# First attention of a two-block model: the value products of two macros issued together every second step, out of four buffers of turned tiles

## What is computed

```python
def forgetting_attention_mixer(h, w_q, w_o, k, v, log_f_cum):
    q = (h @ w_q).reshape(b_sz, t_len, FOX_HEADS, FOX_HD).transpose(0, 2, 1, 3)
    for blk in range(t_len // FOX_QBLOCK):              # four blocks of 128 queries
        s = jnp.einsum("bhqd,bhkd->bhqk", q[:, :, s0:e], k[:, :, :e]) * scale
        s = s + log_f_cum[:, :, s0:e, None] - log_f_cum[:, :, None, :e]
        p = jax.nn.softmax(jnp.where(mask, s, -jnp.inf), axis=-1)
        outs.append(jnp.einsum("bhqk,bhkd->bhqd", p.astype(v.dtype), v[:, :, :e]))
    return o.transpose(0, 2, 1, 3).reshape(b_sz, t_len, FOX_WIDTH) @ w_o
```

## Time and profile before

| | us |
|---|---|
| median of 3 runs (lowest to highest) | 1696.85 (1696.52 to 1697.41) |
| the profiled execution, its own time | 1696.14 |
| its span, first to last instruction | 1694.3 |
| PE busy | 1669.6 (99%) |
| DVE / ACT / POOL busy | 585.4 / 652.6 / 689.0 |
| steps 2 to 19 of the first attention (start of S(2) to start of the tile of step 20) | 863.69 to 928.24 |

### The profile page before, as it was taken

The page is one execution under the profiler, slowest core; times in us unless marked ns, Lnnn a source line. Parts: engine busy times, 40 slices in busy tenths (PEclk is TensorE's granted clock), DMA queues, the critical chain, the costliest instruction groups (busy, mean ns, idle before and its releaser), DMA issues.

```text
span 1694.3 us, 23544 instructions
## 1 busy us (share of the span) xinstructions
PE 1669.6 (99%) x9382; PEld 1401.0 (83%) x9382; DVE 585.4 (35%) x1173; ACT 652.6 (39%) x987; POOL 689.0 (41%) x538
## 2 busy tenths in 40 slices
PE   6999999999999999999999999999999999999999
PEld 6787889898888888897977898888888887887887
DVE  3459325440100001411256230100011536788661
ACT  4653624442222222522456342222222545544651
POOL 3533333434444455535322434544455433554002
PEclk9999999999999999999999999999999999999999
DMA  5212110422222322232120222222322222222001
GB/s 199 75 64 87 51 53 23 162 76 99 99 99 99 111 98 88 75 137 100 52 98 2 75 75 99 84 98 93 125 99 99 100 100 99 75 95 80 26 2 50
DMA packets 23427, 145.00 MB, mean 86 GB/s; under 512 B 3504, under 2 KB 4272, under 8 KB 7344
## 3 DMA queue, kind: packets, MB, share of 16 engines
q1 hardware_dynamic: 23344, 143.83, 24.2%
HBM read 141.72 MB, written 2.10 MB: 85 GB/s over the span
## 4 chain that ended last, share of the span: by engine, by line
PE 68%; issue 13%; POOL 10%; DVE 5%; ACT 2%; DMA 1%; SPq 0%; POOLq 0%; ACTq 0%; DVEq 0%
POOL wlo L2839 10%; PE PS L452 5%; PE PS L454 5%; PE PS L453 5%; PE PS L485 4%; PE PS L343 4%; PE PS L346 4%; PE PS L338 4%; PE PS L487 4%; PE PS L486 4%; PE PS L961 2%; PE PS L466 2%; PE PS L467 2%; PE PS L468 2%; PE PS L1642 2%
## 5 line engine op out<-in xcount | busy, mean ns | idle before, releaser
L2839 POOL TENSOR_TENSOR wlo<-wraw,whi 128x512 fp32r<-128x512 f32 (+1 forms) x476 | 628.4, 1353 | 903.1 <-ACT whi L145 903.1
L145 ACT ACTIVATE whi<-wraw 128x2048 fp32r<-128x2048 f32 (+1 forms) x119 | 225.7, 1896 | 240.0 <-PE PS L346 182.7
L452 PE MATMUL PS<-hT_hi,whi 128*128 128x512 f32 x704 | 274.0, 389 | 0.0
L453 PE MATMUL PS<-hT_lo,whi 128*128 128x512 f32 x704 | 273.9, 389 | 0.0
L454 PE MATMUL PS<-hT_hi,wlo 128*128 128x512 f32 x704 | 273.9, 389 | 0.0
L1544 DVE TENSOR_TENSOR act_sb<-sil,PS 128x512 f32 x44 | 30.3, 688 | 428.5 <-ACT sil L1519 428.5
L1519 ACT ACTIVATE sil<-PS 128x512 f32<-128x512 f32 x44 | 26.4, 599 | 355.2 <-PE PS L454 335.4
L452 PEld LDWEIGHTS PS<-hT_hi,whi 128*128 128x128 f32 x704 | 132.1, 188 | 27.8 <-issue 0.6
L453 PEld LDWEIGHTS PS<-hT_lo,whi 128*128 128x128 f32 x704 | 132.2, 188 | 27.4
L454 PEld LDWEIGHTS PS<-hT_hi,wlo 128*128 128x128 f32 x704 | 132.1, 188 | 27.4
L485 PE MATMUL PS<-whi,hT_hi 128*128 128x512 f32 (+2 forms) x288 | 112.3, 390 | 0.1
(11 more groups left out here) (412 smaller groups left out, 3036.4 us busy)
## 6 DMA issues: line engine op xcount, KB each, us to landing
wraw<-wpack SPq DMA_DIRECT2D x125, 1024.0 KB, 4.9
gain<-gains SPq DMA_DIRECT2D x10, 512.0 KB, 6.5
x_sb<-x SPq DMA_DIRECT2D x8, 512.0 KB, 6.8
out<-x_sb SPq DMA_DIRECT2D x3, 512.0 KB, 2.6
csb<-consts SPq DMA_DIRECT2D x1, 704.0 KB, 13.4
out<-x_sb SPq DMA_DIRECT2D x2, 256.0 KB, 2.0
vh<-vecs SPq DMA_DIRECT2D x1, 96.0 KB, 6.4
small<-vecs SPq DMA_DIRECT2D x1, 80.0 KB, 11.4
```

The source lines that it names most:

```text
L145: act.activation((whi[q % 2] if static is not None else hi_of_slot(n))[:, w], wraw[q % 2][:, w], ACT.Copy).then_inc(w_hi, 1)
L452: nc.tensor.matmul(o, whi[q][w], hT_hi[:, k, :], start=(k == 0), stop=False)
L453: nc.tensor.matmul(o, whi[q][w], hT_lo[:, k, :], start=False, stop=False)
L2839: p.tensor_tensor(lo[:, a:b], wraw[q][:, a:b], hi[:, a:b].bitcast(F32), ALU.subtract).then_inc(w_lo, 1)
```

## The change

`fpt` has four buffers in place of two. The two new ones lie at 52 and 56 KB of the arena. Step m of PE issues no values where m is even; where m is odd, it issues V(m - 3) and then V(m - 2), without anything between them. A copy into `fpt[m % 4]` waits for V(m - 4). Nothing is added or taken away on any engine; ACT, DVE, POOL and SP keep their order.

```diff
-        fpt = [at(f"fpt{i}", AT_XN + 4 * KB * i, [P, 2, SEQ]) for i in range(2)]
+        fpt = [at(f"fpt{i}", (AT_XN if i < 2 else AT_ARENA + 44 * KB) + 4 * KB * i, [P, 2, SEQ]) for i in range(4)]
...
-                                            fpt[m % 2][:, r, c + j * P:c + (j + 1) * P], start=(j == 0), stop=(j == i))
+                                            fpt[m % 4][:, r, c + j * P:c + (j + 1) * P], start=(j == 0), stop=(j == i))
...
                     for p in self.ended(m - 2):
                         if m <= self.n:
                             self.pe_sums(p)
-                    if 0 <= m - 2 < self.n:
+                    if m % 2 and m >= 3:
+                        self.pe_values(m - 3)
                         self.pe_values(m - 2)
...
             def copy_ready(self, eng, m, r):
                 eng.wait_ge(sem("fx_turned"), 2 * m + r + 1)
-                if m >= 2:
-                    eng.wait_ge(sem("fx_pv"), m - 1)
+                if m >= 4:
+                    eng.wait_ge(sem("fx_pv"), m - 3)
```

More of the change, by code:

```diff
@@ L1883, in act_copy @@
                     self.copy_ready(a, m, 1)
-                    a.activation(fpt[m % 2][:, :, :], PS[:, self.turned[0]:self.turned[0] + 2, :], ACT.Copy).then_inc(sem("fx_pt_a"), 1)
+                    a.activation(fpt[m % 4][:, :, :], PS[:, self.turned[0]:self.turned[0] + 2, :], ACT.Copy).then_inc(sem("fx_pt_a"), 1)
                 if self.copies[m] == "av":
                     self.copy_ready(a, m, 0)
-                    a.activation(fpt[m % 2][:, 0, :], PS[:, self.turned[0], :], ACT.Copy).then_inc(sem("fx_pt_a"), 1)
+                    a.activation(fpt[m % 4][:, 0, :], PS[:, self.turned[0], :], ACT.Copy).then_inc(sem("fx_pt_a"), 1)
             def dve_copy(self, m):
@@ L1892, in dve_copy @@
                     self.copy_ready(v, m, 1)
-                    v.tensor_copy(fpt[m % 2][:, :, :], PS[:, self.turned[0]:self.turned[0] + 2, :]).then_inc(sem("fx_pt_v"), 1)
+                    v.tensor_copy(fpt[m % 4][:, :, :], PS[:, self.turned[0]:self.turned[0] + 2, :]).then_inc(sem("fx_pt_v"), 1)
                 if self.copies[m] == "av":
                     self.copy_ready(v, m, 1)
-                    v.tensor_copy(fpt[m % 2][:, 1, :], PS[:, self.turned[1], :]).then_inc(sem("fx_pt_v"), 1)
+                    v.tensor_copy(fpt[m % 4][:, 1, :], PS[:, self.turned[1], :]).then_inc(sem("fx_pt_v"), 1)
             def act_high(self, p):
```

## The result

| | before | after |
|---|---|---|
| median of 6 runs each, us | 1697.09 (1696.31 to 1700.91) | 1703.04 (1702.13 to 1705.87) |
| ratio after to before | | 1.003, 95% interval 1.002 to 1.004 |
| span of the profiled execution, us | 1694.3 | 1702.1 |
| steps 2 to 19, start of S(2) to start of the tile of step 20 | 64.55 | 70.57 |
| start of that tile to the turned sums of step 21 | 8.88 | 8.46 |

A forecast was written before the change was run, and what follows sets the result against it. PE's own queue was taken to set the time, with ACT and DVE chains nearly as late. 7.92 - 1.66 - 0.28 = +5.98 us on 1696.14 gives 1702.1, plus 0.7 for the median: 1702.8 us, range 1699.5 to 1705.8.

The forecast's parts named there:

- what comes back: Even steps 2 to 18: how much earlier the next waiting PE block can start; 1.66 us in sum.
- The price of a value block: Odd steps 3 to 19: a value block directly behind another costs PE 0.88 us, 7.92 for nine.
- The saving per merge: Each of ten merges saves 1.03 - 0.88 = 0.15 us of form changes if nobody waited, 1.5 us in all.
- The chain to the turns: Steps 10 and 12: scores, maximum, exponential, ACT's copy, turns is at its limit; 0 us comes back.
- The spread: Steps 4, 6, 14, 16: next scores start 0.15 us behind DVE's copy of the sums; 0.08 or 0.21 back each.
- DVE's copy at steps 8 and 18: Turns there start 0.15 us behind DVE's copy of the macro before; 0.45 us comes back each.
- The end: Steps 20 and 21: value block leaves between turns and tile, one joins step 21; -0.28 us.
- The forms winning: Rival, attention: turns follow earlier, so form changes and small waits are saved; 1695.2 us, chance 0.06.
- given back by shorter chains: Rival, even steps: some chains shorter than read, 0.4 to 0.5 us more per step back; 1698.8 us, chance 0.11.
- The late values: Rival: late values hold up DVE's finals ahead of the maxima, at most +2.8 us; 1705.6 us, chance 0.08.
- The clock: Rival: long waits in steps 4, 10, 12, 14 bring half clock, 6.4 us; 1709 us, chance 0.05.

The follow-up runs named there:

- e7_last_pair: Kernel before, with only the last two value blocks merged in step 21: steps 2 to 19 64.54 us, end 8.47, ratio 0.9997.
- e5_copy_ahead: Changed kernel, with ACT's half copies ahead of the next macro's exponentials instead of behind them: steps 2 to 19 take 68.58 us.
- e4_short_spread: Changed kernel, with DVE's copy of the turned sums cut from 512 to 128 columns: steps 2 to 19 take 68.99 us.
- e2_two_new: Changed kernel's order of values, but with the old two buffers and the old copy wait: steps 2 to 19 take 70.56 us, end 8.46.
- e6_even_steps: Changed kernel, with double value blocks in even steps 4 to 20 and none in odd steps 3 to 19: steps 2 to 19 70.15 us, end 9.66.

## Why the prediction was right

The forecast was +5.98 us. From start of S(m) to start of S(m + 2), even m, the kernels differ by

| bare step | forecast (0.88 less what comes back) | measured |
|---|---|---|
| 2 | 0.70 | 0.70 |
| 4, 14 | 0.80 | 0.80, 0.80 |
| 6, 16 | 0.67 | 0.64, 0.64 |
| 8, 18 | 0.43 | 0.34, 0.35 |
| 10 | 0.88 | 0.87 |
| 12 | 0.88 | 0.87 |
| 20 and 21 | -0.28 | -0.42 |

(Read from the trace before rounding; differences of rows rounded to 0.01 can be off by 0.02.) Steps 2 to 19 were to take 6.26 us more and took 6.02 more.

**The price of a value block.** 0.88 directly behind another was forecast, 0.87 measured in all ten double blocks. The saving per merge, 0.15, is there; it is only far smaller than what each merge gives away. The end of `e7_last_pair` is the place where it can be seen without a wait beside it. The Trainium skill (page "TensorEngine Tiling (Array Packing)", section "Key Properties") states that a change of tiling mode drains TensorE. The trace agrees in so far as each change of form costs PE time, 0.14 us.

**The chain to the turns.** T(10) is 4.83 to 4.84 us behind S(10) with one value block between them, with none, and with one computed for nothing. `e5_copy_ahead` shows that the copy on ACT closed that chain. The prediction's reading of it was too coarse: turns wait by halves. This did not touch the forecast, since in the old order of ACT the copy, which both halves need, is last anyway.

**The spread.** Steps 4, 6, 14 and 16: the start 0.15 us behind DVE's copy was the middle of two far bounds, and it is what was measured (877.25 against 877.10). `e4_short_spread` shows the wait to be this one, against the profile's own row.

**DVE's copy at steps 8 and 18** left a little less cost than forecast, 0.34 and 0.35 for 0.43. T(8) starts close behind its copy:

```profile
892.38 1.22 DVE L1894 COPY fpt<-PS 128x1024 f32<-128x1024 f32 x1
```
```profile
893.71 1.06 PE L1826 MATMUL PS<-csb,fp 128*128 128x128 f32 x8 [0.54 <-DVE fpt L1894]
```

It starts 0.11 us behind the copy's end, where 0.15 was taken (0.04), and after a wait the block of turns is 0.03 shorter, 1.06 in place of 1.09; the value block gives the last 0.01.

**The end** was sized with turns and tile in one form at 0.88 from start to start. In the changed kernel they take 0.79, and the two tiles are another 0.05 us shorter than the sum had them:

```profile
939.28 1.03 PE L1826 MATMUL PS<-csb,fp 128*128 128x128 f32 x8
940.07 0.71 PE L338 MATMUL PS<-whi,hT_hi 128*128 128x512 f32 x2
```

The miss of the end and those at steps 8 and 18 have the same sign, 0.14 and 0.17 us, and are most of the 0.38 by which the trace's 5.60 lies under the sum of 5.98. The medians give 5.95, which is nearer than the sum deserves: they can't tell 0.4 us.

**The rivals.** The forms winning would have needed the turns to follow; they did not. Nothing was given back by shorter chains: S(10) to T(10) is equal to 0.01 us. The late values did not hold DVE: no step is longer than forecast, and `e2_two_new`, in which copies wait in addition, is equal. (The prediction's remark that PE is through V(m - 2) ahead of T(m - 1) is off by one: it is ahead of T(m), which is all that the copy needs.)

The clock stayed at 1.00 in steps 2 to 19 with single idle times of up to 1.1 us and 7.7 us in all. The Trainium skill tells of a kernel whose clock went to and fro with small idle times (page "TensorE: Matmul & The Clock Gate", section "A second HAM failure mode: psum-queue depth-cycling"). This kernel does not show that. The stretches at half clock in the first 230 us are there in kernels with the old order as well, and none lies in the attention of any kernel here. Nor was the pairing of the earlier trace rows a sign of danger: at the same instruction the changed kernel stood still for 1.31 us and the clock held (timeline, and window of PE), while no idle time stood ahead of the stretch at 57 us.

```profile
191.95 0.50 PE L575 MATMUL PS<-hT_lo,whi 128*128 128x512 f32 x1 [1.31 <-issue]
192.00:195.00 3.00, 3.00 (x13) 1.00 0.02 5
```

## What to carry to other kernels

Before a block is moved on the busiest engine, ask what the others do while it runs: for each place it leaves, look up when the next waiting instruction could start at the earliest, and count only what lies between that time and now. PE was 99% busy here, and yet two other chains were within 0.05 to 0.6 us of it at each step, so bunching equal work gained 0.15 us a time and uncovered 0.5 to 1.0. Where a gap is to be closed, shorten or reorder the chain that ends there first (here the copy ahead of the exponentials), and bunch only where nobody waits.

## What the runs showed of the hardware

- A wait row names one releaser of several. "ACT fp" stood for a wait on DVE; shortening DVE's copy from 0.69 to 0.29 us moved the scores by 0.40 and the name changed to DVE. In this case a distance of 0.15 us behind an instruction's end, equal at all four places, was the better evidence.
- The price of a change of form between runs of matmuls was steady here, 0.15 us with leaving and entering together at each of nine merges. At turns followed by a tile of 512 columns the step inside a form was shorter than expected (0.79 us for eight turns).
- Where PE waited for a copy, it started 0.05 us behind the end of one on ACT, about 0.1 behind DVE's copy of 1024 columns (T(8) and T(18)) and 0.15 behind DVE's copy of 512 (S(5), S(7), S(15), S(17)). Only the turns of step 2 start later behind DVE's copy, 0.26 us, or 0.29 in `e6_even_steps`; they do so in every kernel looked at, and why stays open.
